# Gate factors of a gated linear recurrence, formed per leaf of eight tokens in place of per token

## The chip, the cores and the metric

The kernel runs on one core of one Trainium2 chip. The metric is the device time of one execution in microseconds (us), from the whole network's inputs in memory to its output.

## The reference, cut to what matters

Two small transformer-like blocks follow each other. The first layer of the first block holds a gated linear recurrence of four heads with 128 channels, over 512 latent and 256 context tokens, forwards and backwards. All that the change touches is inside `gla_chunked`:

```
def step(state, inp):
    qc, kc, vc, gc = inp
    b = jnp.cumsum(gc, axis=2)
    diff = b[:, :, :, None, :] - b[:, :, None, :, :]
    decay = jnp.where(prefix_mask, jnp.exp(jnp.minimum(diff, 0.0)), 0.0)
    scores = jnp.einsum('bhtk,bhsk,bhtsk->bhts', qc, kc, decay)
    out = (jnp.einsum('bhtk,bhkv->bhtv', qc * jnp.exp(b), state)
           + jnp.einsum('bhts,bhsv->bhtv', scores, vc))
    b_last = b[:, :, -1:, :]
    new_state = (jnp.exp(b_last[:, :, 0, :])[..., None] * state
                 + jnp.einsum('bhsk,bhsv->bhkv', kc * jnp.exp(b_last - b), vc))
    return new_state, out
```

A score between a query token t and a key token s needs the factor exp(b[t] - b[s]) in every channel, where b is the running sum of the log gates. All the rest (modulations, projections, attention, feed-forward layers) is large matrix products.

## The kernel before

The engines run programs of their own and are ordered by semaphores; the order of every engine's work is written out by hand. Channels lie on the 128 partitions, tokens run along the columns. Four heads are worked in two rounds (`hgrn(0)` and `hgrn(1)`) of two heads each. A round first makes its projections (`win0` or `win1`, ten weight chunks on TensorE), then goes through six recurrent steps. A step takes 256 tokens (two chunks of 128) of two heads in one direction, so that one operand tensor is 128 partitions x 512 columns (2 heads x 256 tokens).

To use plain matmuls for the scores, exp(b[t] - b[s]) is written as exp(b[t] - b[r]) times exp(b[r] - b[s]) with a token r between s and t. For tokens in different halves of a group of 2m tokens, r is the middle of the group; `LEVELS` holds m = 64, 32, 16 and 8. For tokens in the same group of `LEAF` = 8, r is a token in the middle of the leaf. The operands of step n lie in `WK[:, n % 2]`: four level tensors (slots 0 to 3), in which one half of each group is query times factor and the other half key times factor, and LQ, LK (the leaf's queries and keys) and LD (keys decayed to the chunk's end), seven in all. The work of step n:

- POOL, `differences(r, n)`: for each level two subtractions over half of all tokens (L2382, L2383 forwards, L2385, L2386 backwards, 128x256 each, eight in all), then one of 128x512 for the leaves (L2397). Before step n it waits until TensorE has read the same slots in step n - 2 (`spent`). POOL also makes the low parts of the split weights (`split_lo`, L469).
- ACT, `exps(n, 0)`: one exponential over the four level tensors at once (L1959, 128x2048). `exps(n, 1)`: exponentials for LK and LQ (L1961, L1962), LD (L1967, four of 128x128) and two more (L1971, L1977). In between it copies a row of modulation sums out of PSUM (`mod_row`, L1896). In each loop of n it first copies the turned keys of step n (`turned_keys`, L1950), then works on step n + 2.
- DVE, `operands(n)`: eight products of 128x256 for the levels (L2609), then four of 128x512 for LQ, LK, LD and QB (L2614).
- TensorE, `scores(n)`: the score sums FINEST (level m = 8, L1425), WIDER (the other levels, L1438), the transposes of LD (L1446), and last LEAVES (L1425 again). After it in program order: `mod_sums` (L1361, matmuls for the modulation of later layers, which share the time of the steps), `outputs(n - 1)` (L1471, L1474), `updates(n)` (L1458), `mod_turn` (L1371).
- DVE, `mask_scores(n)`: takes FINEST (L2625), WIDER and LEAVES (L2627) out of PSUM through masks, in this order; then `results(n - 1)` (L2656, L2658), `states(n)` (L2642, L2644) and `mod_column` (L2520).

DVE's order in the loop over n is `operands(n + 1)`, `mask_scores(n)`, `results(n - 1)`, `states(n)`, `mod_column`. The score sums use a ring of four PSUM banks, three sums a step, numbered 3n, 3n + 1, 3n + 2; the transposes and the turned modulation sums use bank 5 by turns. Sum u may start when sum u - 4 has been taken. After the steps TensorE goes on with the next projection (`first_chunks`, L851 to L853); its inputs are split by ACT (`part_high`, L945) and POOL (`part_low`, L951).

## Time and profile before

| | |
|---|---|
| median of 3 runs | 2432.0 us (2430.31 to 2433.66) |
| profiled execution, its own time | 2423.83 us |
| its span, from first to last instruction | 2421.7 us |
| TensorE busy | 2311.4 us, 95% |
| DVE busy | 1170.0 us, 48% |
| POOL busy | 974.8 us, 40% |
| ACT busy | 868.9 us, 36% |
| steps of round 0, of round 1 | 135.4 to 202.4 us, 296 to 363 us |

Busy time is the union of an engine's instructions. TensorE's matmuls are pipelined, so a matmul's duration is longer than the spacing of two of them. Durations in the timeline of consecutive instructions of one kind are merged: "2.77 ... x8" is eight instructions in 2.77 us. "[3.06 <-ACT arena L1959]" says that the engine was idle for 3.06 us before the row and that ACT's work of line 1959 ended the wait.

### The profile page before, as it was taken

What the parts mean: (1) busy time and instruction counts of PE and PEld (TensorE: products, weight loads), DVE (VectorE), ACT (ScalarE), POOL (GpSimd) and SP (SyncE); (2) the same over time, 40 slices, a digit from 0 to 9 for tenths busy, and PEclk for the clock granted to TensorE, in tenths of its full rate; (3) what the DMA queues carried; (4) which work ended last, traced back from release to release, by engine and by line L of the source; (5) the groups of instructions that cost most, each with busy time, mean ns of one, the idle gap of its engine ahead of it and who ended that gap; (6) DMA issues with size and microseconds to landing.
All of it is one profiled execution on the core that took longest, in us unless ns stands there. A gap on an engine that the chain in (4) does not pass through costs nothing.

```text
span 2421.7 us, 36690 instructions
## 1 busy us (share of the span) xinstructions
PE 2311.4 (95%) x14013; PEld 1932.8 (80%) x14013; DVE 1170.0 (48%) x1873; ACT 868.9 (36%) x1399; POOL 974.8 (40%) x770
## 2 busy tenths in 40 slices
PE   6989989999999999999999999999999999999997
PEld 3878879888888888898877787778887886688766
DVE  4685681547777753343232346654232006670273
ACT  5444343341111122335224343222443225542452
POOL 2464563333333432333512145655664440154302
PEclk9989989999999999999999999999999999999999
DMA  7131232126555531112200024553223321122212
GB/s 287 66 115 69 72 122 84 53 93 203 183 196 191 184 104 61 61 61 91 64 1 1 18 87 156 183 197 110 98 89 116 97 87 47 55 76 90 66 45 70
DMA packets 64438, 245.11 MB, mean 101 GB/s; under 512 B 7168, under 2 KB 8448, under 8 KB 63552
## 3 DMA queue, kind: packets, MB, share of 16 engines
q1 hardware_dynamic: 64080, 242.67, 29.0%
q8 instruction: 84, 1.38, 0.2%
q0 software_dynamic: 240, 0.79, 0.1%
q14 instruction: 34, 0.28, 0.0%
HBM read 241.33 MB, written 2.10 MB: 101 GB/s over the span
## 4 chain that ended last, share of the span: by engine, by line
PE 73%; DVE 4%; issue 3%; ACT 3%; POOL 2%; DVEq 0%; POOLq 0%; ACTq 0%
PE ps L851 13%; PE ps L852 13%; PE ps L853 13%; PE ps L1554 4%; PE ps L1556 4%; PE ps L1557 4%; PE ps L612 2%; PE ps L1802 1%; PE ps L1789 1%; PE ps L1726 1%; POOL w_low L469 1%; PE ps L888 1%; PE ps L890 1%; PE ps L889 1%; ACT arena L2302 1%
## 5 line engine op out<-in xcount | busy, mean ns | idle before, releaser
L469 POOL TENSOR_TENSOR w_low<-ring,w_high 128x512 fp32r<-128x512 f32 (+2 forms) x534 | 752.0, 1430 | 1138.8 <-ACT w_high L460 1132.3
L460 ACT ACTIVATE w_high<-ring 128x1024 fp32r<-128x1024 f32 (+2 forms) x267 | 274.7, 1031 | 957.1 <-PE ps L853 638.8
L851 PE MATMUL ps<-h_high,w_high 128*128 128x512 f32 x1040 | 412.0, 396 | 17.1 <-POOL h_low L714 7.3
L852 PE MATMUL ps<-h_low,w_high 128*128 128x512 f32 x1040 | 407.4, 392 | 0.0
L853 PE MATMUL ps<-h_high,w_low 128*128 128x512 f32 x1040 | 407.0, 391 | 0.0
L851 PEld LDWEIGHTS ps<-h_high,w_high 128*128 128x128 f32 x1040 | 196.6, 189 | 70.9 <-issue 13.2
L853 PEld LDWEIGHTS ps<-h_high,w_low 128*128 128x128 f32 x1040 | 196.4, 189 | 41.7
L852 PEld LDWEIGHTS ps<-h_low,w_high 128*128 128x128 f32 x1040 | 196.8, 189 | 38.0
L2839 DVE TENSOR_TENSOR hidden<-arena,hidden 128x1536 fp32r<-128x1536 f32 (+1 forms) x42 | 87.2, 2077 | 193.3 <-ACT hidden L2098 193.3
L1554 PE MATMUL ps<-hidden,w_high 128*128 128x512 f32 (+1 forms) x504 | 178.6, 354 | 0.0
L1556 PE MATMUL ps<-hidden,w_high 128*128 128x512 f32 (+1 forms) x504 | 178.5, 354 | 0.0
L1557 PE MATMUL ps<-hidden,w_low 128*128 128x512 f32 (+1 forms) x504 | 178.3, 354 | 0.0
L2528 DVE CUSTOM_DVE_ANT_0 const<-const,arena 128x1024 f32<-128x1024 f32 x96 | 160.5, 1700 | 28.7 <-DMA const<-late_w_dram 28.7
L853 PE MATMUL ps<-h_ctx_high,w_low 128*128 128x256 f32 x376 | 106.4, 283 | 0.0
L852 PE MATMUL ps<-h_ctx_low,w_high 128*128 128x256 f32 x376 | 106.4, 283 | 0.0
L851 PE MATMUL ps<-h_ctx_high,w_high 128*128 128x256 f32 x376 | 106.3, 283 | 0.0
L1554 PEld LDWEIGHTS ps<-hidden,w_high 128*128 128x128 f32 x504 | 95.3, 189 | 13.4
L1556 PEld LDWEIGHTS ps<-hidden,w_high 128*128 128x128 f32 x504 | 95.3, 189 | 13.2
L1557 PEld LDWEIGHTS ps<-hidden,w_low 128*128 128x128 f32 x504 | 95.3, 189 | 13.2
L2302 ACT ACTIVATE arena<-arena 128x512 f32<-128x512 f32 (+2 forms) x128 | 81.0, 634 | 61.9 <-DVE arena L2993 61.8
L2786 DVE TENSOR_TENSOR arena<-ps,arena 128x512 f32 (+1 forms) x65 | 38.8, 598 | 102.6 <-PE ps L853 101.8
L2733 DVE SCALAR_TENSOR_TENSOR XB<-ps,mod,XB 128x512 f32<-128x512 f32 (+1 forms) x40 | 27.9, 697 | 107.3 <-PE ps L853 96.4
(465 smaller groups left out, 4868.6 us busy)
## 6 DMA issues: line engine op xcount, KB each, us to landing
const<-late_w_dram SPq DMA_DIRECT2D x112, 512.0 KB, 5.0
ring<-up_dram SPq DMA_DIRECT2D x88, 512.0 KB, 3.3
ring<-down_dram SPq DMA_DIRECT2D x44, 512.0 KB, 3.2
ring<-winE_dram SPq DMA_DIRECT2D x32, 512.0 KB, 3.5
XB<-ada_dram SPq DMA_DIRECT2D x20, 768.0 KB, 5.4
ring<-win_dram SPq DMA_DIRECT2D x20, 512.0 KB, 3.2
ring<-winC_dram SPq DMA_DIRECT2D x20, 512.0 KB, 3.5
arena<-ada_dram SPq DMA_DIRECT2D x12, 768.0 KB, 20.9
```

The costliest lines, as they stand in the source:

```text
L460: nc.scalar.activation(WH[p][:, 0:L], RAW[p][:, 0:L], ACT.Copy).then_inc(w_hi, 1)
L469: ins = nc.gpsimd.tensor_tensor(WL[p][:, to], RAW[p][:, to], WH[p][:, to].bitcast(F32), ALU.subtract)
L612: ins = nc.tensor.matmul(bank[:, at + g * t:at + g * t + g], src[:, t * P:(t + 1) * P], ones, start=(begins and j == tiles_[0] and t == 0) ...
L851: nc.tensor.matmul(bank[:, 0:n], wh[:, cols], hi, start=(k == 0), stop=False)
L852: nc.tensor.matmul(bank[:, 0:n], wh[:, cols], lo, start=False, stop=False)
L853: ins = nc.tensor.matmul(bank[:, 0:n], wl[:, cols], hi, start=False, stop=(k == kt - 1))
L1554: MM(to, wh[:, cols], hi, start=start and m % per == 0 and j == 0, stop=False, skip_group_check=True)
L1556: MM(to, wh[:, cols], lo, start=False, stop=False, skip_group_check=True)
L1557: ins = MM(to, wl[:, cols], hi, start=False, stop=stop and j == 1, skip_group_check=True)
L2302: A(at, at, ACT.Exp, scale=-1.0, bias=column(NM, kind, u, x), accum_out=column(LSUM, kind, u, x)).then_inc(e_p, 1)
L2528: nc.vector.tensor_tensor_reduce(LATE_W[t], LATE_W[t], vectors[x + t], 1.0, 0.0, ALU.mult, ALU.add, LATE_SUM[:, x + t:x + t + 1]).then_inc ...
L2839: TT(lo, inner_pair(c, width, i), hi.bitcast(F32), ALU.subtract).then_inc(g_lo, 1)
```

## The change

The factor of a level is now made of two parts: the leaf's own factor, which is there for LQ and LK anyway, and one factor for each leaf and level, exp of the difference between the leaf's middle token and the group's middle. These are 32 values a head for each level (`EDGE`, 2 x 4 x 2 x 32 columns that lay unused behind the constants). So POOL first subtracts for the leaves (one 128x512), then makes eight subtractions of 128x32. ACT takes the exponentials for LK and LQ first, then one over 128x256 of `EDGE`. DVE first makes LK and LQ, waits for its own semaphore, and then makes the level tensors as products of these with `EDGE`, each value repeated over eight tokens. The scores are taken in the order LEAVES, FINEST, WIDER, transposes, and the sums are numbered in this order (`SCORE_ORDER`); `mask_scores` still goes FINEST, WIDER, LEAVES. `hg_ops` counts three marks a step. The wait in `differences` is now for the LEAVES sum of step n - 2 and for DVE's second mark of that step. In step 0 the split of weight chunk 8 comes after the leaf subtraction and before the small ones. Left out below: the definitions of `EDGE` and `score_sum`, and waits whose numbers only follow.

```
+        def leaves(ap, m, second):
+            v = ap.rearrange("p h c n -> p (h c n)").rearrange("p (g y e) -> p g y e", y=2 * m // LEAF, e=LEAF)
+            return v[:, :, m // LEAF:, :] if second else v[:, :, 0:m // LEAF, :]
+        def edges(w, l, m, second):
+            v = EDGE[:, w, l, :, :].rearrange("p h x -> p (h x)").rearrange("p (g y) -> p g y", y=2 * m // LEAF)
+            v = v[:, :, m // LEAF:] if second else v[:, :, 0:m // LEAF]
+            return v.unsqueeze(3).to_broadcast([*v.shape, LEAF])
...
-                    pe.wait_ge(hg_ops, 2 * (6 * r + n) + 1)
...
+                    pe.wait_ge(hg_ops, 3 * (6 * r + n) + 1)
+                    full(LEAVES, LK, LQ)
+                    pe.wait_ge(hg_ops, 3 * (6 * r + n) + 2)
                     full(FINEST, NL - 1, NL - 1)
...
+                    pe.wait_ge(hg_ops, 3 * (6 * r + n) + 3)
...
-                    full(LEAVES, LK, LQ)
...
                     if x == 0:
-                        levels = WK[:, w, 0:NL, :, :, :].rearrange("p a h c n -> p (a h c n)")
-                        A(levels, levels, ACT.Exp).then_inc(hg_exp, 1)
+                        act.wait_ge(hg_diff, 2 * done + 1)
+                        A(wk(w, LK), wk(w, LQ), ACT.Exp, scale=-1.0)
+                        A(wk(w, LQ), wk(w, LQ), ACT.Exp)
+                        act.wait_ge(hg_diff, 2 * done + 2)
+                        edge = EDGE[:, w, :, :, :].rearrange("p l h x -> p (l h x)")
+                        A(edge, edge, ACT.Exp).then_inc(hg_exp, 1)
                         return
-                    A(wk(w, LK), wk(w, LQ), ACT.Exp, scale=-1.0)
-                    A(wk(w, LQ), wk(w, LQ), ACT.Exp)
...
+                if n >= 2:
+                    await_sums(pool, f"hgS{r}", score_sum(n - 2, LEAVES))
+                elif r:
+                    await_sums(pool, "hgS0", score_sum(n + 4, LEAVES))
+                if 6 * r + n >= 2:
+                    pool.wait_ge(hg_ops, 3 * (6 * r + n - 2) + 2)
...
+                TT(wk(w, LQ).rearrange("p h (x e) -> p h x e", e=LEAF), by_leaf,
+                   mids.to_broadcast([P, 2, CTX // LEAF, LEAF]), ALU.subtract).then_inc(hg_diff, 1)
                 if between:
                     split_lo(*between)
...
+                for l, m in enumerate(LEVELS):
+                    g, y = CTX // (2 * m), m // LEAF
...
+                    for second in (False, True):
+                        part = slice(y, 2 * y) if second else slice(0, y)
+                        x, mine = to[:, :, :, part], mid_of[:, :, :, part]
+                        ins = TT(x, mine, at, ALU.subtract) if second == (d == 0) else TT(x, at, mine, ALU.subtract)
+                ins.then_inc(hg_diff, 1)
...
                     dve.wait_ge(hg_exp, 2 * done + 1)
+                    TT(wk(w, LK), wk(w, LK), k, ALU.mult)
+                    TT(wk(w, LQ), wk(w, LQ), q, ALU.mult).then_inc(hg_ops, 1)
+                    dve.wait_ge(hg_ops, 3 * done + 1)
                     for l, m in enumerate(LEVELS):
-                        x = wk(w, l)
                         for second in (False, True):
-                            f = q if second == (d == 0) else k
-                            ins = TT(half(x, m, second), half(x, m, second), half(f, m, second), ALU.mult)
+                            whole = WK[:, w, LQ if second == (d == 0) else LK, :, :, :]
+                            ins = TT(leaves(WK[:, w, l, :, :, :], m, second), leaves(whole, m, second),
+                                     edges(w, l, m, second), ALU.mult)
                     ins.then_inc(hg_ops, 1)
                     dve.wait_ge(hg_exp, 2 * done + 2)
-                    for to, f in ((wk(w, LQ), q), (wk(w, LK), k), (wk(w, LD), k),
-                                  (QB[:, n % 3, :, :, :].rearrange("p h c n -> p h (c n)"), q)):
+                    for to, f in ((wk(w, LD), k), (QB[:, n % 3, :, :, :].rearrange("p h c n -> p h (c n)"), q)):
```

## Rows read from the trace of the kernel before

**Rows 1.** The page: busy time of the engines.

```profile
PE 2311.4 (95%) x14013; PEld 1932.8 (80%) x14013; DVE 1170.0 (48%) x1873; ACT 868.9 (36%) x1399; POOL 974.8 (40%) x770
```

**Rows 2.** Busy time by stretch: steps of both rounds, then two single periods.

```profile
135.40:202.40 67.00, 56.19 (x696) 46.90 (x695) 58.20 (x109) 30.16 (x58) 40.03 (x45) 0.90 0.35 125
296.00:363.00 67.00, 56.34 (x696) 46.92 (x694) 58.35 (x109) 31.54 (x61) 40.14 (x45) 0.90 0.36 133
...
160.72:174.10 13.38, 10.54 (x118) 8.55 (x118) 12.89 (x23) 5.71 (x11) 8.15 (x12) 0.85 0.32 119
186.60:195.62 9.02, 8.67 (x118) 7.28 (x118) 8.57 (x21) 5.06 (x8) 4.26 (x4) 1.00 0.06 14
```

**Rows 3.** Waits of TensorE, 117 to 200 us: total, times, longest.

```profile
PE ps L1446 <- DVE mod L2520: 5.4, 4, 2.2
PE ps L1438 <- DVE arena L2625: 2.0, 2, 1.4
PE ps L1361 <- ACT arena L1896: 1.8, 1, 1.8
```

**Rows 4.** Timeline of DVE in round 0: start, us, line.

```profile
135.97 2.77 DVE L2609 TENSOR_TENSOR arena<-arena 128x256 f32<-128x256 f32 x8
...
141.06 0.69 DVE L2625 TENSOR_TENSOR arena<-ps,const 128x512 f32<-128x512 f32 x1
141.78 1.51 DVE L2627 COPY_PREDICATED arena<-const,ps 128x512 f32<-128x512 uint32 x2
...
147.71 6.25 DVE L2609 TENSOR_TENSOR arena<-arena 128x256 f32<-128x256 f32 x8 [3.06 <-ACT arena L1959]
...
160.72 6.51 DVE L2609 TENSOR_TENSOR arena<-arena 128x256 f32<-128x256 f32 x8
...
174.10 5.66 DVE L2609 TENSOR_TENSOR arena<-arena 128x256 f32<-128x256 f32 x8
...
186.60 2.77 DVE L2609 TENSOR_TENSOR arena<-arena 128x256 f32<-128x256 f32 x8
...
192.41 1.54 DVE L2627 COPY_PREDICATED arena<-const,ps 128x512 f32<-128x512 uint32 x2
```

**Rows 5.** Timeline of POOL in round 0.

```profile
115.94 2.54 POOL L469 TENSOR_TENSOR w_low<-ring,w_high 128x512 fp32r<-128x512 f32 x2
...
131.76 1.03 POOL L2397 TENSOR_TENSOR arena<-arena 128x512 f32<-128x512 f32 x1
138.30 3.32 POOL L2382 TENSOR_TENSOR arena<-arena 128x256 f32<-128x256 f32 x1 [5.51 <-PE ps L1438]
141.58 0.62 POOL L2383 TENSOR_TENSOR arena<-arena 128x256 f32<-128x256 f32 x1
142.16 0.61 POOL L2382 TENSOR_TENSOR arena<-arena 128x256 f32<-128x256 f32 x1
...
161.11 0.80 POOL L2382 TENSOR_TENSOR arena<-arena 128x256 f32<-128x256 f32 x1
```

**Rows 6.** Timeline of TensorE in round 0.

```profile
118.54 0.50 PE L851 MATMUL ps<-squares_rounded,w_high 128*128 128x512 f32 x1 [0.62 <-POOL w_low L469]
...
182.19 1.14 PE L1425 MATMUL ps<-arena 128*128 128x128 f32 x8
...
186.83 0.63 PE L1446 MATMUL ps<-const,arena 128*128 128x128 f32 x4 [1.78 <-DVE mod L2520]
...
192.64 1.14 PE L1425 MATMUL ps<-arena 128*128 128x128 f32 x8
...
202.41 0.48 PE L851 MATMUL ps<-squares_rounded,w_high 128*128 128x512 f32 x1
```

**Rows 7.** Timeline of ACT in round 0.

```profile
145.77 1.91 ACT L1959 ACTIVATE arena<-arena 128x2048 f32<-128x2048 f32 x1 [6.33 <-POOL arena L2383]
...
147.95 0.62 ACT L1961 ACTIVATE arena<-arena 128x512 f32<-128x512 f32 x1
...
148.99 1.26 ACT L1967 ACTIVATE arena<-arena 128x128 f32<-128x128 f32 x4
```

More of the change, by code:

```diff
@@ L49 @@
 FINEST, WIDER, LEAVES = range(SCORE_SUMS)
+SCORE_ORDER = (LEAVES, FINEST, WIDER)
 LAM_INIT = 0.8 - 0.6
@@ L999, in step_mods, with score_sum @@
             return FIRST_MODS + ROUND_MODS * r + n
+        def score_sum(n, x):
+            return SCORE_SUMS * n + SCORE_ORDER.index(x)
         def keys_sum(n):
@@ L1418, in scores @@
                     w = n % 2
-                    pe.wait_ge(hg_ops, 2 * (6 * r + n) + 1)
                     def full(x, ka, qa):
-                        bank = open_bank(pe, SS, SCORE_SUMS * n + x).rearrange("p (h c t) -> p h c t", h=2, c=2)
+                        bank = open_bank(pe, SS, score_sum(n, x)).rearrange("p (h c t) -> p h c t", h=2, c=2)
                         for h in range(2):
@@ L1426, in full @@
                                                        start=True, stop=True)
-                        sums_done(ins, SS, SCORE_SUMS * n + x)
+                        sums_done(ins, SS, score_sum(n, x))
+                    pe.wait_ge(hg_ops, 3 * (6 * r + n) + 1)
+                    full(LEAVES, LK, LQ)
+                    pe.wait_ge(hg_ops, 3 * (6 * r + n) + 2)
                     full(FINEST, NL - 1, NL - 1)
                     back = STEPS[n][0]
-                    bank = open_bank(pe, SS, SCORE_SUMS * n + WIDER).rearrange("p (h c t) -> p h c t", h=2, c=2)
+                    bank = open_bank(pe, SS, score_sum(n, WIDER)).rearrange("p (h c t) -> p h c t", h=2, c=2)
                     for l, m in enumerate(LEVELS[:NL - 1]):
@@ L1440, in scores @@
                                                            skip_group_check=True)
-                    sums_done(ins, SS, SCORE_SUMS * n + WIDER)
-                    pe.wait_ge(hg_ops, 2 * (6 * r + n) + 2)
+                    sums_done(ins, SS, score_sum(n, WIDER))
+                    pe.wait_ge(hg_ops, 3 * (6 * r + n) + 3)
                     bank = open_bank(pe, SK, keys_sum(n)).rearrange("p (h c t) -> p h c t", h=2, c=2)
@@ L1955, in exps @@
                     w, done = n % 2, 6 * r + n
-                    act.wait_ge(hg_diff, 2 * done + x + 1)
                     if x == 0:
-                        levels = WK[:, w, 0:NL, :, :, :].rearrange("p a h c n -> p (a h c n)")
-                        A(levels, levels, ACT.Exp).then_inc(hg_exp, 1)
+                        act.wait_ge(hg_diff, 2 * done + 1)
[4 more added lines that the diff above has]
+                        A(edge, edge, ACT.Exp).then_inc(hg_exp, 1)
                         return
-                    A(wk(w, LK), wk(w, LQ), ACT.Exp, scale=-1.0)
-                    A(wk(w, LQ), wk(w, LQ), ACT.Exp)
                     b = tok(A_b[d], chunks)
@@ L2002, in hgrn @@
                         act.wait_ge(h_ready, KT)
-                        await_sums(act, SS, SCORE_SUMS * 4 + LEAVES)
+                        await_sums(act, SS, score_sum(4, WIDER))
                         part_high(r + 1, 0, range(4))
                     if n == 5:
-                        await_sums(act, SS, SCORE_SUMS * 5 + LEAVES)
+                        await_sums(act, SS, score_sum(5, WIDER))
                         await_sums(act, SU, 10)
@@ L2364, in differences @@
                 w = n % 2
-                def spent(x):
-                    if n >= 2:
-                        await_sums(pool, f"hgS{r}", SCORE_SUMS * (n - 2) + x)
-                    elif r:
-                        await_sums(pool, "hgS0", SCORE_SUMS * (n + 4) + x)
-                spent(WIDER)
+                if n >= 2:
+                    await_sums(pool, f"hgS{r}", score_sum(n - 2, LEAVES))
+                elif r:
+                    await_sums(pool, "hgS0", score_sum(n + 4, LEAVES))
@@ L2373, in differences @@
+                if 6 * r + n >= 2:
+                    pool.wait_ge(hg_ops, 3 * (6 * r + n - 2) + 2)
                 pool.wait_ge(hg_b, 2 * r + d + 1)
                 b = tok(A_b[d], chunks)
-                for l, m in enumerate(LEVELS):
-                    x = wk(w, l)
-                    g = CTX // (2 * m)
-                    at = b.rearrange("p h (g x) -> p h g x", x=2 * m)[:, :, :, m - 1 + d:m + d]
-                    at = at.to_broadcast([P, 2, g, m])
-                    early, late = half(b, m, False), half(b, m, True)
-                    if d == 0:
-                        TT(half(x, m, False), at, early, ALU.subtract)
-                        ins = TT(half(x, m, True), late, at, ALU.subtract)
-                    else:
-                        TT(half(x, m, False), early, at, ALU.subtract)
-                        ins = TT(half(x, m, True), at, late, ALU.subtract)
@@ L2387, in differences @@
-                ins.then_inc(hg_diff, 1)
+                by_leaf = b.rearrange("p h (x e) -> p h x e", e=LEAF)
+                mid = LEAF // 2 - 1 + d
+                mids = by_leaf[:, :, :, mid:mid + 1]
+                TT(wk(w, LQ).rearrange("p h (x e) -> p h x e", e=LEAF), by_leaf,
+                   mids.to_broadcast([P, 2, CTX // LEAF, LEAF]), ALU.subtract).then_inc(hg_diff, 1)
                 if between:
                     split_lo(*between)
-                spent(LEAVES)
-                def blocks(y, m):
-                    return y.rearrange("p h (g x) -> p h g x", x=m)
```

14 lines of the change are left out of this document (7 added, 7 removed).

## The prediction, made before the change was run

> **What bounds the kernel now.** The page comes first. TensorE is busy for 2311.4 us, 95% of the span [rows 1]. So time can only be won where TensorE idles or runs slowly. The change touches the recurrent steps, so the next view is the one by stretches, over the six steps of each of the two rounds [rows 2]. In 67.0 us TensorE is busy for 56.2 and 56.3, so it idles for 10.8 and 10.7, and its mean granted clock is 0.90. DVE is busy for 58.2 and 58.4. The two rounds agree to 0.2 us, so I work out one and double it.
>
> The waits of TensorE in these steps lead to DVE (5.4 us for the transposes' bank, 2.0 for a score bank) and 1.8 to an ACT copy that is queued behind the exponentials [rows 3]. DVE's own timeline shows who sets the pace [rows 4]. Call "block n" the products of step n (L2609, then L2614). Blocks 1 and 5, when POOL has nothing to do, take 2.77 us for the eight L2609; blocks 2, 3 and 4 take 6.25, 6.51 and 5.66. POOL's timeline says why [rows 5]: at 161.11, inside block 3, its subtractions run one by one between DVE's products and are stretched themselves, from 0.61 us to 0.80. At 138.30 it is the other way: a subtraction is held for 3.32 us, until block 1 is done. The 0.69 us mask product that reads PSUM is not slowed [rows 4]. So products of two SBUF tensors and POOL's subtractions exclude each other, and that exclusion is the cost in these steps. The Trainium skill ("GPSIMD Engine Reference", section Key points) says the same, that the SBUF interfaces are shared with Vector instructions of two SBUF inputs; the trace agrees, with 2.77 against 6.51 us.
>
> **The stretch that is summed.** I take the end of the mask of step 0, 143.29 us (141.78 + 1.51), and of step 4, 193.95 (192.41 + 1.54), 50.66 us apart [rows 4]. From the mask of step 4 to the first matmul after the steps (202.41, [rows 6]) are 8.5 us of scores, outputs and states. There the LEAVES score (about 1.1 us, as the one at 182.19) leaves the end of the chain, but FINEST now waits for the mask of step 4, so I count this tail as unchanged.
>
> **The change, part by part.**
>
> *POOL.* Eight subtractions of 128x256 become eight of 128x32; the 128x512 one stays and comes first. The large ones cost 0.58 us each from start to start (141.58 to 142.16), the 128x512 one 1.03 [rows 5]. A line through these two leaves about 0.15 us that does not depend on size, so a small one is estimated at 0.15 + 0.05 = 0.20 us, between 0 and 0.58. Per step: 1.0 + 8 x 0.20 = 2.6 us in place of at least 1.0 + 8 x 0.58 = 5.6. The Trainium skill ("GPSIMD Engine Reference", Elementwise side-by-side cycle accounting) gives 2.6 cycles an element at 1.2 GHz and no fixed part in that rate; by it a small one would be an estimated 0.07 us, and as this work is mostly hidden, the forecast would move by under 1 us a round.
>
> *ACT.* One exponential of 128x2048 at 1.91 us becomes one of 128x256, between the 0.32 us of a 128x128 (1.26 / 4) and the 0.62 of a 128x512 [rows 7]. That saves some 1.5 us a step, hidden, except at step 2: there block 2 waited 3.06 us for L1959 [rows 4]. Now POOL may start after the LEAVES score, which is first, and its result is ready about 2.6 + 1.0 us later, before the states of step 0 are through. That idle goes, and with it TensorE's 1.8 us on ACT [rows 3].
>
> *DVE.* The same twelve products over the same number of elements: two of 512 columns, eight of 256 with one factor repeated over eight columns, two of 512. I price the repeated factor at nothing (the mask product repeats a factor too, at 0.69 us for 512 columns); bounds 0 and 0.1 us for each. New is a wait for the engine's own semaphore between the first two products and the eight. Bounds: 0.03 us, the gap ahead of 141.78, and 0.35, a whole product (2.77 / 8), if none overlapped the next [rows 4]; I take 0.2 us a step.
>
> *TensorE.* The same matmuls in another order, LEAVES, FINEST, WIDER, transposes. By the ring of four banks FINEST now waits until the whole mask of the step before is taken. Behind it queue WIDER, the transposes, the ada sums and the outputs; DVE comes to WIDER only after the next block, and the transposes' bank is waited for anyway (1.78 us at 186.83, [rows 6]), so this wait takes the place of another. TensorE's work in one full-clock step is 10.45 us from FINEST to FINEST less 1.78 of idle, 8.67 us [rows 6], under the pace that DVE sets below. Its idle falls to about a tenth, so I expect the full 2.4 GHz level to hold where it now falls: the mean is 0.85 between 160.72 and 174.10 [rows 2].
>
> *Start of the round.* The split of weight chunk 8 on POOL comes ahead of the small subtractions. Now it ends at 118.48 and TensorE waits 0.62 us for it [rows 5, 6]; it should end some 4 us sooner. The gain is 0.6 us a round.
>
> **The sum for a round.** The eight products of blocks 2, 3 and 4 are longer than those of block 1 by 3.48, 3.74 and 2.89 us, 10.1 together. The idle ahead of block 2 is 3.06 [rows 4]. The new wait costs 0.2 in each of blocks 1 to 5, -1.0. With 0.6 from the start that is 12.8 us. The starts of blocks 2 to 5 are now 13.0, 13.4 and 12.5 us apart; they would be 9.7, 9.8 and 9.8.
>
> From this goes what POOL still takes from DVE. In block 3 the products that alternate cost (6.51 - 2.77) / 8 = 0.47 us more each, against a subtraction of 0.58 [rows 4, 5], so DVE loses about POOL's time less 0.1: 0.9 for the large one, 0.1 for a small one. In block 1 they overlap, because POOL is released by LEAVES of step 0 just when block 1 starts: 0.9 + 8 x 0.1 = 1.7 us. For steps 3 to 5 POOL is released by the LEAVES score, the last of TensorE's 8.7 us of a step, about when DVE has come to the next mask, which does not exclude it; I take 0.4 us for all three. That leaves 12.8 - 2.1 = 10.7 us a round, 21 us in all. The profiled execution took 2423.8 us (span 2421.7), so it would take 2403; the median of the runs is 2432.0, 0.34% above it, and what is saved is the same: 2411 us. No change that can be told from none is 0.2%, 5 us.
>
> **The rivals.**
>
> *A, the forecast:* exclusion nearly gone, 8.5 to 12.8 us a round: 2407 to 2415. Chance 0.60.
>
> *B, something else holds the steps:* the clock still falls or TensorE becomes the bound. Between 160.72 and 174.10 TensorE needed 10.54 us busy at a mean clock of 0.85 [rows 2]; if that is the period in place of 9.8, and block 1 loses 3.7 instead of 1.7, the round gains 10.7 - 3 x 0.7 - 2.0 = 6.6. With half of today's exclusion left (10.1 / 2) in place of 0.4, and block 1 as in the forecast, it is 6.1, and with both of them 2. So 2417 to 2428, around 2419. For it: TensorE's work of 8.67 us leaves it 1.1 us of slack only. Against: the period from 186.60 to 195.62 is just 9.0 us with no fall of the clock [rows 2]. Chance 0.23.
>
> *C, TensorE gets all of it:* all idle (10.8) and the slow clock (56.2 busy at 0.90, of which some 5 us would go) are recovered, 13 to 15 us a round: 2402 to 2406. For it: DVE would have to wait for nothing and the wait in each block cost nothing. Against: DVE's periods of 9.8 stay above 8.7. Chance 0.09.
>
> *D, slower:* the small subtractions exclude DVE for as long as the large ones did, since the exclusion is by instruction and not by size. The price is 0.47 us each, so 0.9 + 8 x 0.47 = 4.7 in a block. If all four blocks 1 to 4 meet it, block 1 included, which POOL now leaves alone, a round loses 18.6 and gains 12.8: 6 us slower, 12 for both, 2444. It decides if POOL's start drifts into each block and the price is over (12.8 / 4 - 0.9) / 8 = 0.29 us each. Against it: the POOL instruction held at 138.30 cost DVE nothing, and LEAVES comes late in the period. Chance 0.04.
>
> *E, no change:* the steps speed up, but the split parts that POOL makes for the next stage end no earlier, or the price in D is near 0.29. Their chain starts from ACT's copies in step 4 and moves with it, and after the steps TensorE goes straight on at 202.41 [rows 6]. Chance 0.04.
>
> **The numbers.** Faster is A + B + C, 0.92, same 0.04, slower 0.04. The likeliest time is 2411. The range leaves out D, E and the far ends of B and C: 2403 to 2423; A's own is 2407 to 2415.
>
> **What would show it.** The eight level products at about 2.8 us in blocks 2 to 4 (the step right) or above 5 (D). The starts of blocks 3, 4 and 5 some 9.8 us apart. TensorE idle in the steps down from 10.8 to 3 us or less, granted clock near 1.00. POOL's small subtractions near 0.2 us. No 0.62 us wait at 118. DVE's idle ahead of block 2 gone. It would be wrong if a repeated factor costs DVE time, if POOL's start falls into the blocks, or if TensorE waits for FINEST's bank longer than it now waits for the transposes'.

## The result, and the profile after

The changed kernel takes 2410.4 us (median of four runs, 2406.9 to 2414.0) where the one before takes 2432.4 beside it (four runs): 22 us less, a ratio of 0.991 with an interval of 0.9893 to 0.9928. The forecast was 2411 us, with a range of 2403 to 2423, so the time is the forecast's (rival A). How much of that closeness is luck is said below, after the sum. The profiled execution took 2410.65 us, its span is 2408.5. The page's first row answers to [rows 1]: each engine but TensorE is busy for less, and TensorE for 2.7 us more.

```profile
PE 2314.1 (96%) x14013; PEld 1935.4 (80%) x14013; DVE 1159.7 (48%) x1873; ACT 851.9 (35%) x1399; POOL 938.1 (39%) x770
```

The view by stretches shows round 0: the steps, from 0.6 us ahead of block 1 up to the first matmul of the next projection as in [rows 2], and then three parts of them: from mask 0 to mask 4, and two single periods. Columns: us, busy time of PE, PEld, DVE, ACT and POOL, mean granted clock (1.00 is full speed), share of the DMA engines, GB/s.

```profile
140.49:196.96 56.47, 51.69 (x696) 43.61 (x696) 50.10 (x109) 22.83 (x54) 26.44 (x45) 1.00 0.42 156
149.90:188.30 38.40, 35.90 (x476) 29.68 (x476) 36.21 (x83) 17.38 (x41) 11.24 (x26) 1.00 0.26 98
161.15:171.12 9.97, 8.97 (x134) 7.41 (x130) 9.44 (x22) 4.11 (x11) 4.62 (x13) 1.00 0.42 160
171.12:180.87 9.75, 9.32 (x132) 7.76 (x128) 9.22 (x23) 4.10 (x11) 0.00 (x0) 1.00 0.01 2
```

The stretch that the sum was made over, from the end of the mask of step 0 to that of step 4, is now 38.4 us long and not 50.7. In it TensorE idles for 2.5 us and its granted clock is 1.00, the 2.4 GHz level, throughout. Over all six steps of round 0, which take 56.5 us in place of 67.0, its idle is 56.47 - 51.69 = 4.8 us in place of 10.8 [rows 2]; the prediction had 3 us or less as its sign.

TensorE's waits over 124 to 197 us answer to [rows 3]:

```profile
PE ps L1442 <- DVE arena L2641: 4.3, 5, 1.8
PE ps L1490 <- DVEq L2663: 0.4, 1, 0.4
```

The waits for the transposes' bank, for WIDER and for ACT are gone. One large one is left: L1442, the line of LEAVES and FINEST, here FINEST, for the masks of L2641. DVE's timeline answers to [rows 4]; L2617 and L2618 make LK and LQ, L2623 the level products, L2628 LD and QB, L2639 and L2641 are the masks.

```profile
141.09 0.68 DVE L2617 TENSOR_TENSOR arena<-arena 128x512 f32<-128x512 f32 x1
...
142.40 4.06 DVE L2623 TENSOR_TENSOR arena<-arena,const 128x256 f32<-128x256 f32 x8
...
148.41 1.50 DVE L2641 COPY_PREDICATED arena<-const,ps 128x512 f32<-128x512 uint32 x2
...
151.50 0.69 DVE L2617 TENSOR_TENSOR arena<-arena 128x512 f32<-128x512 f32 x1 [0.24 <-DVE arena L2658]
...
152.83 2.77 DVE L2623 TENSOR_TENSOR arena<-arena,const 128x256 f32<-128x256 f32 x8
...
161.15 0.81 DVE L2617 TENSOR_TENSOR arena<-arena 128x512 f32<-128x512 f32 x1
...
162.70 2.77 DVE L2623 TENSOR_TENSOR arena<-arena,const 128x256 f32<-128x256 f32 x8
...
171.12 0.68 DVE L2617 TENSOR_TENSOR arena<-arena 128x512 f32<-128x512 f32 x1
171.72 0.68 DVE L2618 TENSOR_TENSOR arena<-arena 128x512 f32<-128x512 f32 x1
172.44 2.77 DVE L2623 TENSOR_TENSOR arena<-arena,const 128x256 f32<-128x256 f32 x8
175.13 1.29 DVE L2628 TENSOR_TENSOR arena<-arena 128x512 f32<-128x512 f32 x2
176.34 0.68 DVE L2639 TENSOR_TENSOR arena<-ps,const 128x512 f32<-128x512 f32 x1
```

The eight level products take 2.77 us in blocks 2, 3 and 4, where they took 6.25, 6.51 and 5.66, and the 3.06 us of idle ahead of block 2 are gone. Block 1 alone is longer, 4.06 in place of 2.77. POOL's timeline, which answers to [rows 5], shows what it collides with:

```profile
120.71 1.92 POOL L2408 TENSOR_TENSOR const<-arena 128x32 f32<-128x32 f32 x8
...
141.68 1.58 POOL L2396 TENSOR_TENSOR arena<-arena 128x512 f32<-128x512 f32 x1 [7.89 <-PE ps L1442]
143.23 3.39 POOL L2408 TENSOR_TENSOR const<-arena 128x32 f32<-128x32 f32 x8
...
149.30 1.93 POOL L2408 TENSOR_TENSOR const<-arena 128x32 f32<-128x32 f32 x8
...
159.00 1.04 POOL L2396 TENSOR_TENSOR arena<-arena 128x512 f32<-128x512 f32 x1 [7.77 <-PE ps L1442]
160.00 2.83 POOL L2408 TENSOR_TENSOR const<-arena 128x32 f32<-128x32 f32 x8
...
168.03 1.04 POOL L2396 TENSOR_TENSOR arena<-arena 128x512 f32<-128x512 f32 x1 [5.20 <-PE ps L1442]
```

POOL runs inside block 1 (141.68 to 146.6) and then at 148.3 to 151.2, just ahead of block 2; the work that starts at 159.0 still reaches into the start of block 3, and from 168.0 on it lies beside the end of the mask, the results and the state updates.

**Where the 22 us come from.** The next table adds up both traces by the same marks (all from the timelines, in us): the start of the first weight product of the first projection, the end of the mask of step 0 and of step 4 in each round, and the first matmul after the steps. "After, again" is the same kernel in another execution, run with the experiments.

| | before | after | after, again |
|---|---|---|---|
| start to first weight product | 44.65 | 50.67 | 50.13 |
| from there to mask 0, round 0 | 98.65 | 99.24 | 99.21 |
| mask 0 to mask 4, round 0 | 50.65 | 38.42 | 38.39 |
| mask 4 to the end of the steps | 8.46 | 8.64 | 8.64 |
| next projection, to mask 0, round 1 | 101.32 | 101.95 | 102.05 |
| mask 0 to mask 4, round 1 | 50.75 | 38.68 | 42.03 |
| mask 4 to the end of the steps | 8.47 | 8.64 | 8.64 |
| all from the first weight product | 318.30 | 295.56 | 298.95 |
| from there to the end | 2058.8 | 2062.3 | 2067.7 |

The part that the change touches is 22.7 us shorter, as much as the medians differ. The two profiled executions themselves differ by 13.2 us only, as the start was 6.0 us later in the second and the rest 3.5 us longer. The change edits nothing in either part, and whether it moves them all the same stays open for the start (taken up at the end). And round 1 is not the same in every execution: 38.7 and 42.0 us. That was not in the prediction, and experiments 1 and 7 are about it.

### The profile page after: what moved, and what is told of

Read it like the earlier page. It is cut to its first block, busy times and chain, and to the rows that moved or that the text cites. A ratio compares the mean times of both kernels' runs of the same rounds, so it can differ in the third digit from the quotient of the medians.

```text
span 2408.5 us, 36702 instructions
## 1 busy us (share of the span) xinstructions
PE 2314.1 (96%) x14013; PEld 1935.4 (80%) x14013; DVE 1159.7 (48%) x1873; ACT 851.9 (35%) x1399; POOL 938.1 (39%) x770
## 4 chain that ended last, share of the span: by engine, by line
PE 73%; DVE 3%; issue 3%; ACT 3%; POOL 2%; DVEq 0%; POOLq 0%; ACTq 0%
PE ps L852 14%; PE ps L853 13%; PE ps L854 13%; PE ps L1573 4%; PE ps L1575 4%; PE ps L1576 4%; PE ps L613 2%; PE ps L1821 1%; PE ps L1808 1%; POOL w_low L470 1%; PE ps L1745 1%; PE ps L889 1%; PE ps L890 1%; PE ps L891 1%; ACT arena L2322 1%
## 5 line engine op out<-in xcount | busy, mean ns | idle before, releaser
L852 PEld LDWEIGHTS ps<-h_high,w_high 128*128 128x128 f32 x1040 | 197.0, 189 | 69.2 <-issue 12.2
L1573 PEld LDWEIGHTS ps<-hidden,w_high 128*128 128x128 f32 x504 | 95.3, 189 | 13.2
L1808 PEld LDWEIGHTS ps<-const,arena 128*128 128x128 f32 x352 | 38.3, 143 | 51.4 <-ACT arena L2322 25.7
```

Of the source, the lines that this page charges most:

```text
L852: nc.tensor.matmul(bank[:, 0:n], wh[:, cols], hi, start=(k == 0), stop=False)
L1573: MM(to, wh[:, cols], hi, start=start and m % per == 0 and j == 0, stop=False, skip_group_check=True)
L1808: ins = nc.tensor.transpose(bank[:, j * P:(j + 1) * P], probs[:, j * P:(j + 1) * P], ident)
```

## The experiments

Each kernel is the changed one with the edit shown, and each ratio is to the kernel before on the same chip. "Stretch" is the table's row from the first weight product to the end of the second steps; for the kernel before and, but for round 1's first period, for the changed one it repeats within 0.3 us, for experiments 7 and 8 together within 0.9, and it is the sharper measure. Its way to mask 0 has most of that scatter (98.2 and 98.8 us for 7 and 8 together); from mask 0 to mask 4 of round 0 each kernel that was traced twice repeats within 0.03 us.

**1. Both kernels once more.** No edit.

> The kernel before, once more with a profile. In the two profiles so far the first weight product of the first projection starts at 44.65 us before the change and at 50.67 after, and nothing that the change touches runs earlier. Theory 1 (this is scatter from run to run, from the moment at which TensorE's clock first rises): the start lies anywhere from 44 to 51 us here, while the stretch from the mask of step 0 to that of step 4 is again 50.6 to 50.8 us in both rounds. Theory 2 (the change delays the start): it is 44.65 again within 0.5 us.

> The kernel after, once more. Theory 1 (the steps give 11.4 us a round and nothing else changes): 2410 us within 3, mask 0 to mask 4 in 38.4 to 38.7 us in both rounds; the start of the first projection may differ from 50.67 by several us. Theory 2 (the change delays the start by 6 us): the start is 50.67 again within 0.5.

The kernel before took 2424.0 us in one run, with a stretch of 318.1; each part up to the end of the steps, the start among them (44.94), is within 0.3 us of the table. The changed one took 2409.2 (2403.6 to 2418.6), ratio 0.9913 (0.9886 to 0.9941). Its stretch, 299.0, is in the table's last column, 19.2 us shorter than 318.1. Its start, 50.13, is within 0.54 us of the first. So each kernel repeated its own start and theory 2, a start that the change delays, isn't ruled out by these runs. The periods from mask to mask in round 1 are 12.5, 10.0, 9.7 and 9.8 us where round 0 has 9.0, 9.8, 9.7 and 9.8. TensorE's waits in 284 to 345 us name the cause, a transfer of modulation weights:

```profile
PE ps L1379 <- DMA XB<-ada_dram: 2.9, 2, 2.4
PE ps L1442 <- DVE arena L2641: 2.3, 3, 1.0
```

Behind that sum (L1379) queue the state updates of step 0 on TensorE (L1477), and DVE waits for them. After the wait TensorE also runs slowly for a while, at a granted clock of 0.50, the 1.2 GHz level:

```profile
298.00:301.00 3.00, 3.00 (x15) 2.49 (x12) 0.78 (x3) 2.27 (x7) 0.00 (x0) 0.50 0.65 190
```

DVE's timeline of the same execution:

```profile
300.63 0.49 DVE L2656 COPY arena<-ps 128x128 f32<-128x128 f32 x2 [2.22 <-PE ps L1477]
...
302.00 0.69 DVE L2617 TENSOR_TENSOR arena<-arena 128x512 f32<-128x512 f32 x1 [0.24 <-DVE arena L2658]
302.61 1.53 DVE L2618 TENSOR_TENSOR arena<-arena 128x512 f32<-128x512 f32 x1
304.18 3.40 DVE L2623 TENSOR_TENSOR arena<-arena,const 128x256 f32<-128x256 f32 x8
```

In round 0 the idle at this place is 0.22 us, L2618 takes 0.68 and the eight L2623 2.77. So the period is longer by 2.0 us of idle, and by 0.85 + 0.63 us because block 2, now late, meets POOL's subtractions: 3.5 us, which is the whole of 12.5 - 9.0. In the kernel before the same transfer made TensorE wait in round 1 too (284 to 350 us):

```profile
PE ps L1361 <- DMA XB<-ada_dram: 1.6, 2, 0.9
```

But its first period was 15.33 us against 15.22 in round 0: the wait lay under the idle ahead of block 2, which the change removed. The late transfer is the usual case. Of the eight traces with the change and the old slots (the two of the table, experiments 2 to 6 and 8), seven have a first period of 12.2 to 12.9 us in round 1, and the first profiled execution with its 9.45 is the exception.

**2. Give POOL its time back.** Eight subtractions of 128x256 on buffers that nobody reads come behind POOL's own in steps 2 to 5. Work is added, nothing left out.

```
+                if n >= 2:
+                    for j in range(8):
...
+                        TT(scrap[:, k % 2, :], const[:, 0:2 * P], const[:, 0:2 * P], ALU.subtract).then_inc(extra, 1)
```

> The kernel after, but after each step's own subtractions, for which nobody waits longer, POOL makes eight more of 128x256 from the constants into a scrap tensor (steps 2 to 5 of each round; the result is used by nobody). Theory 1 (what was won is that POOL no longer excludes DVE's products): the extra ones alternate with DVE in blocks 2 to 4 as before the change, 0.47 us each, blocks 2, 3 and 4 grow by 2 to 4 us each, 6 to 11 a round, so 2422 to 2432 us. Theory 2 (what was won is the shorter chain from POOL over ACT to DVE and the earlier start): that chain is as short as before, so 2410 to 2413.

It took 2427.2 us (2420.8 to 2432.2, ten runs), ratio 0.9985 (0.9968 to 1.0001): nearly all of the gain is gone. The stretch is 314.1, 15.1 us longer than that of the changed kernel in experiment 1, which is 15.1 of its 19.2 us of gain. DVE's timeline, blocks 2 to 4, then POOL's beside block 4:

```profile
152.89 3.38 DVE L2630 TENSOR_TENSOR arena<-arena,const 128x256 f32<-128x256 f32 x8
...
164.10 4.07 DVE L2630 TENSOR_TENSOR arena<-arena,const 128x256 f32<-128x256 f32 x8
...
176.07 5.69 DVE L2630 TENSOR_TENSOR arena<-arena,const 128x256 f32<-128x256 f32 x8
```

```profile
173.35 2.84 POOL L2409 TENSOR_TENSOR const<-arena 128x32 f32<-128x32 f32 x8
176.16 6.08 POOL L2416 TENSOR_TENSOR scrap<-const 128x256 f32<-128x256 f32 x8
```

Nobody waits for the results of these subtractions; the next step's own lie behind them in POOL's queue, no more. Yet the same eight products of DVE go from 2.77 to 5.69 us where the large subtractions (0.76 us each in the second fence's last row) lie beside them. Nor does DVE wait for them by another way: from mask 0 to mask 4 in round 0 no idle of it is longer than 0.24 us, as in the changed kernel. TensorE's mean granted clock there falls to 0.89, but DVE doesn't wait for TensorE either, so the slower clock did not make the periods longer. The exclusion is shown.

**3. Make the factors late instead.** The rival reason for the gain: not POOL's time beside DVE, but that the factors are ready sooner. Four copies of `EDGE` on ACT, each waiting for the one before, hold the mark that DVE waits for.

```
-                        A(edge, edge, ACT.Exp).then_inc(hg_exp, 1)
+                        ins = A(edge, edge, ACT.Exp)
+                        for j in range(4):
+                            ins.then_inc(extra, 1)
+                            act.wait_ge(extra, 4 * done + j + 1)
+                            ins = A(edge, edge, ACT.Copy)
+                        ins.then_inc(hg_exp, 1)
```

> The kernel after, with four more passes of ACT over the leaf factors (copies in place, 128x256, each waiting for the one before) ahead of the mark that DVE waits for. That gives back the 1.5 to 2 us of exponentials that the change took from ACT in every step. Theory 1: hidden, 2410 to 2412, and the blocks 2 to 5 start as late after the masks as before. Theory 2 (the shorter exponential is what was won): 5 blocks of 2 rounds by 1.5 to 2 us, 2425 to 2430.

It took 2410.7 us (2402.3 to 2421.1), ratio 0.9916 (0.9885 to 0.9946), and the stretch is 298.99 against 298.95. ACT's timeline has the copies, 1.77 us a step:

```profile
145.87 0.42 ACT L1982 ACTIVATE const<-const 128x256 f32<-128x256 f32 x1 [0.17 <-POOL const L2414]
146.32 1.77 ACT L1986 ACTIVATE const<-const 128x256 f32<-128x256 f32 x4
```

So the factors may come 1.8 us later for nothing; that much slack, but no more, is shown. Ahead of block 2 DVE idles for no longer than before the edit, so with the rest of the change in place the shorter exponentials earned nothing.

**4. The order of before.** FINEST, WIDER, transposes, LEAVES, with the factored operands kept.

```
-SCORE_ORDER = (LEAVES, FINEST, WIDER)
+SCORE_ORDER = (FINEST, WIDER, LEAVES)
```

(and the calls in `scores` in this order.)

> The kernel after with the old order of the scores on TensorE (FINEST, WIDER, transposes, LEAVES), so that POOL, which must not overwrite the leaf tensors before LEAVES has read them, starts about 4 us later in a period, inside DVE's next block. Theory 1 (exclusion of POOL and DVE): its 2.6 to 3 us of subtractions now fall into blocks 2 to 4 and cost 1.4 to 1.7 us each, 4 to 5 a round: 2418 to 2421. FINEST no longer waits for the whole mask, which by itself gives nothing. Theory 2 (the order costs nothing, or FINEST's new wait costs): 2407 to 2411.

It took 2413.1 us (2406.1 to 2416.9), ratio 0.9897 (0.9864 to 0.9931). The runs can't tell it from the changed kernel; the stretch is 302.7, 3.7 us longer. That is far less than the 8 us and more that were expected, for two reasons that the trace shows. POOL, released late, leaves block 1 alone: from the first weight product to mask 0 takes 97.7 us in place of 99.2. And the loss in round 1's first period lies under the wait for the transfer (12.4 us there). What is left is POOL in blocks 2 to 4, as DVE's timeline shows for block 3:

```profile
158.92 3.69 DVE L2622 TENSOR_TENSOR arena<-arena,const 128x256 f32<-128x256 f32 x8
```

POOL's 128x512 subtraction (160.71 to 161.92 us) stretches one of these eight to 1.26 us, which is 0.84 of the 0.92 that they lose; a small one costs a tenth of that. Most of the gain is thus the smaller operands', and the order adds 3.7 us of 19.2. Were the transfer in time, the order would be worth more, an estimated 3.7 + (12.37 - 10.59) = 5.5 us, with 10.59 the first period of this kernel's round 0. DVE idles 0.24 us ahead of block 2 here too: the new order isn't needed to take away the 3.06 us.

**5. POOL released by the last score.** The order of the change is kept, and POOL waits for WIDER of step n - 2 where it waited for LEAVES: later by FINEST's wait for its bank and by the two sums, 1.13 and 1.80 us, so by about 3 us at the least. In the release ahead of step 4 the wait was 1.68 us and the sums took 1.92 and 2.47 at a granted clock of 0.55 to 0.65, so part of that delay is the clock's.

```
-                    await_sums(pool, f"hgS{r}", score_sum(n - 2, LEAVES))
+                    await_sums(pool, f"hgS{r}", score_sum(n - 2, WIDER))
```

> The kernel after, but POOL waits for the WIDER sum of step n - 2, as before the change, and no longer for LEAVES; TensorE's order stays. WIDER ends about 2.9 us after a mask's end, some 0.6 us into DVE's next block. Theory 1: POOL's 3 us fall into the block and cost 1.4 to 1.7 us in blocks 2 to 4, 4 to 5 a round: 2418 to 2421. Theory 2 (when POOL works is all the same, as its result is early enough): 2409 to 2411.

It took 2418.6 us (2407.7 to 2423.2, seven runs), ratio 0.9935 (0.991 to 0.9961), stretch 304.2, 5.2 us longer, as theory 1 had it. Block 3 on DVE, and POOL beside it:

```profile
159.43 3.83 DVE L2623 TENSOR_TENSOR arena<-arena,const 128x256 f32<-128x256 f32 x8
```

```profile
160.47 1.29 POOL L2396 TENSOR_TENSOR arena<-arena 128x512 f32<-128x512 f32 x1 [7.22 <-PE ps L1458]
161.72 3.55 POOL L2408 TENSOR_TENSOR const<-arena 128x32 f32<-128x32 f32 x8
```

DVE lost 3.83 - 2.77 = 1.06 us on these eight products, and 0.84 of it to the one subtraction of 128x512, beside which a single product took 1.26 us in place of 0.42; the three small ones that met them cost 0.07 each. Where POOL's work starts in the period matters still, and mostly for the subtraction that the change left as large as it was.

**6. Keep POOL out of block 1.** POOL waits before step 2 until DVE has finished block 1.

```
+                if n == 2:
+                    pool.wait_ge(hg_ops, 3 * (6 * r + 1) + 3)
```

> The kernel after, where POOL in step 2 also waits for DVE's third mark of step 1, so that it no longer meets block 1, which takes 6.6 us against 5.2 for the undisturbed blocks. Theory 1: block 1 goes to 5.2 us, POOL's result and the exponential are ready just as block 2 starts, and a round gains 1.0 to 1.4 us: 2407 to 2408. Rival (the result then comes too late for block 2): what is won in block 1 is given back as idle ahead of block 2, 2410.

It took 2409.9 us (2401.9 to 2412.1), ratio 0.9883 (0.9848 to 0.9919); stretch 295.96, 3.0 us shorter than in experiment 1. Block 1 runs undisturbed (the way to mask 0 is 1.35 us shorter), but in round 0 POOL's work lands in block 2, the first period grows from 9.03 to 9.91 us and the way from mask 0 to mask 4 by 0.64, so 0.7 us are won there. In round 1 the way from mask 0 to mask 4 loses 0.3, and the projection ahead of mask 0 takes 99.4 us in place of 102.1; of that, 1.3 us are more than the undisturbed block can explain, and stay open. The forecast of 2407 to 2408 was missed by the whole time, which scatters too widely to tell 1 us.

**7. The weights earlier.** The two transfers for the first sums of round 1 were issued after the whole projection, because their slots are free only then, while those for the second sums went early into the other two slots. The slots are numbered anew, so that it is the other way round.

```
+        def ada_slot(v):
+            return (v if v < 2 * ROUND_MODS else v + 2) % ADA_SLOTS
...
-            load_mods(range(2 * ROUND_MODS + 2, 2 * ROUND_MODS + 4))
+            load_mods(range(2 * ROUND_MODS, 2 * ROUND_MODS + 2))
...
             await_sums(sp, "win1", 18)
-            load_mods(range(2 * ROUND_MODS, 2 * ROUND_MODS + 2))
-            load_mods(range(2 * ROUND_MODS + 4, 4 * ROUND_MODS))
+            load_mods(range(2 * ROUND_MODS + 2, 4 * ROUND_MODS))
```

> The kernel after, with the weights of the modulation sums of round 1 put into other slots, so that the two chunks which the first sums of the round need are loaded before the end of the projection, as in round 0. In most profiles of the changed kernel the period from the mask of step 0 to that of step 1 is 9.0 us in round 0 and 12.5 in round 1, and TensorE waits there for this transfer. Theory 1 (the steps now start so early that this transfer is late): the period in round 1 falls to 9.0 to 9.5, the steps of round 1 gain 3 us, 2406 to 2407. Rival (the 3 us are from the slow clock or the mask): 12.5 stays.

It took 2408.4 us (2408.0 to 2410.2), ratio 0.9916 (0.99 to 0.9932); stretch 294.8, 4.15 us shorter than in experiment 1. TensorE's waits in 284 to 345 us are now those of round 0:

```profile
PE ps L1445 <- DVE arena L2644: 4.3, 5, 1.8
PE ps L1493 <- DVEq L2666: 0.4, 1, 0.4
```

Round 1's first period is 9.02 us, and mask 0 to mask 4 take 38.39, as in round 0. The transfer, with the slow clock behind it, was the whole of the 3.6 us that round 1 lost from mask 0 to mask 4. The ratio is the changed kernel's; that the whole time gains by it is not shown.

**8. One product moved to POOL.** With POOL nearly idle in the steps, it makes the product for QB, behind the subtractions of the same step and ahead of those of the next; DVE keeps LD. TensorE and ACT wait for a semaphore of it.

```
-                    for to, f in ((wk(w, LD), k), (QB[:, n % 3, :, :, :].rearrange("p h c n -> p (h c n)"), q)):
-                        ins = TT(to, to, f, ALU.mult)
-                    ins.then_inc(hg_ops, 1)
+                    TT(wk(w, LD), wk(w, LD), k, ALU.mult).then_inc(hg_ops, 1)
...
+                TT(to, to, tok(A_q, STEPS[n][1]), ALU.mult).then_inc(hg_qb, 1)
```

> The kernel after, where the product for QB (queries for the state, 128x512) is made by POOL between the subtractions of two steps, and not by DVE. Theory 1 (DVE sets the period of 9.75 us, TensorE needs about 9.3 of it, and POOL's product falls beside the mask, which does not exclude it): DVE's block is 0.6 us shorter, the period goes to 9.2 to 9.4, 1.5 to 2.5 us a round: 2405 to 2407. Rival (the product falls into a block): POOL's 1.03 us cost DVE 0.9 against 0.6 saved, 2411 to 2414.

It took 2407.3 us (2403.3 to 2410.5), ratio 0.9888 (0.9858 to 0.9917). From mask 0 to mask 4 in round 0 are 37.5 us in place of 38.4; the whole stretch is 295.3. DVE does 0.6 us less in each block, but the product costs POOL 1.27 us, and it and the subtractions behind it reach into blocks 2 and 3, so less than half of the 2.4 us came through.

**9. Together.** Experiments 7 and 8 in one kernel, twice, and then 6 with them.

> QB made by POOL and the other slots, together. Theory 1: the two add up, mask 0 to mask 4 in 37.5 us in both rounds (38.4 and 42.0 in the kernel after), 2402 to 2405. Rival (TensorE is the bound once the transfer is early): no more than with the slots alone, 38.4 us.

> QB made by POOL and the other slots once more, since single runs of one program scatter by several us and the four of the first time happened to lie within 3. Both rounds again 37.5 us from mask 0 to mask 4. If the gain over the kernel after is real, 2399 to 2405; if the four runs were luck, around 2408.

> As the one before, and POOL's step 2 also waits for DVE's third mark of step 1. Theory 1: block 1 is 1.3 us shorter in both rounds, and of this 0.4 us a round remain at the end of the steps, since POOL's work for step 3 then begins later: 2401 to 2404. Rival: what block 1 gains is all given back, the same as the one before.

7 and 8 together took 2401.2 us (2399.8 to 2402.7), ratio 0.9883 (0.9867 to 0.99), and the second time 2404.6 (2399.3 to 2407.4), ratio 0.9887 (0.9867 to 0.9907). Their stretches are 293.1 and 292.2 us, against 295.6 and 299.0 of the changed kernel. That beats the kernel before by 27 and 28 us on the same chips. It beats the changed one by its shorter stretch; by the ratios alone it is 0.2 to 0.3% better than the changed one's 0.991, with intervals that overlap, so by the whole time it is likely and not shown. All three together took 2410.1 (2403.5 to 2412.4), ratio 0.9919 (0.9904 to 0.9934): worse than two, against both theories. The stretch, 295.2, is 2.1 to 3.0 us longer than with two; the rest of the 8.9 us between the times of the two kernels on this chip isn't placed. Its periods are 10.6, 10.9, 9.7 and 9.2 us. DVE's block 2 and POOL beside it show why:

```profile
144.83 4.90 DVE L2639 TENSOR_TENSOR arena<-arena,const 128x256 f32<-128x256 f32 x8
```

```profile
145.59 1.47 POOL L2423 TENSOR_TENSOR arena<-arena 128x512 f32<-128x512 f32 x1 [2.69 <-ACT arena L2003]
147.03 1.22 POOL L2404 TENSOR_TENSOR arena<-arena 128x512 f32<-128x512 f32 x1
148.21 3.11 POOL L2416 TENSOR_TENSOR const<-arena 128x32 f32<-128x32 f32 x8
```

POOL, held at step 2, makes QB and the subtractions of step 3 late, right in block 2 and on into block 3. What it gave in block 1 it took back, and more, in the next two: the way to mask 0 is 0.9 to 1.5 us shorter, mask 0 to mask 4 take 40.3 us in place of 37.5.

## Why the prediction was right, step by step

**The exclusion as the cause.** This is right, and is shown by experiment 2 (POOL's time given back alone) and 3 (not the latency). Predicted for mask 0 to mask 4: the 10.1 us of longer products and the 3.06 of idle, less four own waits of 0.2 and 0.4 of remaining contention, 12.0 us; measured 12.2. From mask to mask the periods of steps 2 to 4 are 9.86, 9.75 and 9.78 us; the starts of the blocks were predicted 9.7, 9.8 and 9.8 apart. The 0.47 us for each product, read in block 3, was a mean over two things: beside a subtraction of 128x256 a product loses 0.42, and beside the one of 128x512 behind them 0.84.

**The small subtraction.** Estimated at 0.20 us, measured 1.92 / 8 = 0.24 undisturbed. The Trainium skill ("GPSIMD Engine Reference", Elementwise side-by-side cycle accounting) has a rate per element and no figure for a fixed part, which gave an estimated 0.07 us; the trace, with 0.24 us, does not agree for an instruction this small. As the prediction said, little hung on it.

**ACT.** The exponential of 128x256 takes 0.42 us, between its bounds of 0.32 and 0.62. The idle ahead of block 2 and TensorE's 1.8 us on ACT went. By experiments 3 and 4, where DVE idles 0.24 us there, neither the shorter exponential nor the new order is needed for it; a kernel without both was not run.

**DVE.** The repeated factor costs nothing: 2.77 us for the eight products in either kernel. The engine's own wait was taken as 0.2 us a step. The undisturbed block 4 lasts from 171.12 to 176.34, 5.22 us; block 1 of before from 135.97 to 141.06, 5.09 [rows 4]. So the wait costs 0.13 us.

**TensorE.** FINEST now waits for its bank five times a round, 4.3 us in all, in place of the 5.4 and 2.0 us for banks of before [rows 3]. So the idle of the six steps is 4.8 us, more than the 3 that the prediction allowed. From mask 0 to mask 4 the clock stayed at its 2.4 GHz level in both rounds of the first execution (1.00). Rival B's half of it, a clock that still falls, came only where the transfer was late: 0.94 on average in round 1 of the second. TensorE did not become the bound: it idles 2.5 us in 38.4.

**The start of the round.** No wait for the split of weight chunk 8 is left, and the first product of block 1 starts 141.09 - 50.67 = 90.42 us after the first weight product, where it started 135.97 - 44.65 = 91.32 us after it. That is 0.9 us, not 0.6.

**What POOL still takes.** Block 1: the products from 141.09 to 147.70 last 6.61 us, 1.39 over the undisturbed 5.22, predicted 1.7 (0.9 for the large subtraction, 0.8 for the small ones). The timeline in two windows parts them, the first of the eight level products and the other seven:

```profile
142.40 1.15 DVE L2623 TENSOR_TENSOR arena<-arena,const 128x256 f32<-128x256 f32 x1
...
143.47 2.99 DVE L2623 TENSOR_TENSOR arena<-arena,const 128x256 f32<-128x256 f32 x7
```

Seven undisturbed ones take 2.44 us (block 3). So beside the 128x512 subtraction (141.68 to 143.26) the first product lost 1.15 - 0.42 = 0.73 us, and beside the small ones the others lost (2.99 - 2.44) / 7 = 0.08 each. Block 3: 161.15 to 166.60, 5.45, so 0.23; blocks 2 and 4 nothing; predicted 0.4 for all. Rival D's price of 0.47 for each small subtraction is thus 0.08, a little under the forecast's 0.1 and far below the 0.29 from which D would decide. Its other condition, a meeting in every block, experiments 4 and 5 came near: they lost 3.7 and 5.2 us and stayed faster than before, which agrees with the price.

**The tail.** Counted as unchanged; it is 0.18 us longer in both rounds.

**The sum.** Predicted 10.7 us a round. In the profiled execution round 0 gave 12.23 - 0.59 - 0.18 = 11.5 and round 1 12.07 - 0.63 - 0.17 = 11.3, 22.7 together (22.73 by the stretch), to 21 predicted. In the second execution it was 19.2. That the medians lie 0.6 us from the forecast is in part luck: the single runs of the changed kernel lie up to 15 us apart, and the 21 lies between the gain of an execution without the late transfer and one with it, which the prediction knew nothing of.

**What the prediction did not see.** It doubled round 0. Round 1 has a transfer of weights that ends late by an amount that changes between executions. It was hidden ahead of block 2 as long as DVE idled there anyway, and where it is late, as in seven of eight traces, it takes back up to 3.6 us (42.03 to 38.39). "Costs nothing while X waits" had been asked of ACT and of the banks, and not of the DMA queue. The terms that were set too dear (own wait, block 1, start) made up for some of it. In how many of the four timed runs the transfer was late can't be read, as only one of them has a trace.

## What to carry to other kernels

When two engines slow each other by turns, what shrinking one's work can win is read ahead of any run, as the same instructions' time with and without the neighbour (6.51 against 2.77 us here). Take the price from single instructions and not from a mean, since one large instruction can hide among small ones: here most of what is left is the single 128x512 subtraction. After shrinking, place what is left in the period by its release: a delay of 3 us and more cost 5 us over the two rounds, and holding it back gave 1.35 us in one block and lost 0.64 in the next. Before removing an idle, list everything that hides in it, in every round, transfers above all.

## What the runs showed of the hardware

**The price of a meeting goes with the size of POOL's instruction.** 128x32 subtractions that alternate with DVE's products of 128x256 stretch themselves from 0.24 to 3.39 / 8 = 0.42 us and cost DVE 0.07 to 0.08 each. Those of 128x256 in experiment 2 go from 0.58 to 0.76 and cost DVE (5.69 - 2.77) / 7 = 0.42, as seven of the eight products met one. The one of 128x512 goes from 1.04 to 1.2 to 1.6 and costs DVE 0.73 (block 1) and 0.84 (experiments 4 and 5). Both engines lose, and in each case DVE loses 0.16 to 0.31 us less than the subtraction takes when it runs alone.

**TensorE may start slowly, and the granted clock does not always say so.** TensorE's timeline of before, then of after, the same modulation sums (L1361 and L1379) ahead of the first projection:

```profile
24.94 2.79 PE L1361 MATMUL ps<-arena,cs 128*32 128x384 f32 x16
...
28.70 1.80 PE L1361 MATMUL ps<-arena,cs 128*32 128x384 f32 x16
```

```profile
24.58 2.79 PE L1379 MATMUL ps<-arena,cs 128*32 128x384 f32 x16
...
28.67 2.79 PE L1379 MATMUL ps<-arena,cs 128*32 128x384 f32 x16
```

Before, sixteen matmuls take 1.80 us from 28.70 on; after, the same take 2.79 until 38 us and 2.48 at 42.18, and the projection begins at 50.67 us and not at 44.65. The column of the granted clock reads 1.00 in both. In the second execution of the changed kernel these matmuls ran at full pace from 20.5 to 30 us (0.85 us for eight) and then took 2.79 as well, and here the column reads 0.50. The view of 32 to 40 us, first and second execution, the same work at the same pace and two readings of the clock:

```profile
32.00:40.00 8.00, 8.00 (x41) 5.86 (x42) 0.57 (x4) 1.04 (x4) 0.00 (x0) 1.00 0.81 329
```

```profile
32.00:40.00 8.00, 8.00 (x42) 5.86 (x42) 0.57 (x4) 1.01 (x3) 0.00 (x0) 0.50 0.82 330
```

So what held the engine in the first execution, the column does not record; what it was stays open. Over the fourteen traces the projection began anywhere from 44.4 to 50.7 us. Is that scatter, or the kernel's? The slow matmuls come in different places in two executions of one kernel, yet the start of each kernel that was traced twice came back within 0.8 us: 44.65 and 44.94 before, 50.67 and 50.13 after, 44.38 and 45.11 with experiments 7 and 8 together. The edits leave this part alone, but that the start is free of them is not shown. The part after the steps, which took 2058.8 to 2070.1 us over the traces, does scatter within one kernel, by 5.4 us in the changed one. Single runs of one kernel lie up to 15 and 19 us apart (experiments 1 and 3), and these two parts are the likely reason. So the effects of 1 to 5 us above were read from the stretch and not from the whole time.
